# Layer ends by token halves with weights kept in the arena: a two-block model on one core

## The reference, cut to what matters

```python
def first_block(...):                      # x with 16 meta tokens ahead: 528 tokens
    ...
        h = h + _sq_relu_mlp(_rmsnorm(h, norm_mlp[layer]), mlp_w1[layer], mlp_w2[layer])
    h = _rmsnorm(h, norm_final)
    return h[:, N_META:, :]

def second_block(...):
    for l in range(DEPTH):                 # DEPTH = 2
        x = x + 0.5 * rms_norm(swiglu(rms_norm(x, nw[0]), ffn_w_gate[l, 0], ...), nw[1])
        hn = rms_norm(x, nw[2])
        m = even_mixer(hn, ...) if l % 2 == 0 else odd_mixer(hn, ...)
        x = x + rms_norm(m, nw[3])
        x = x + 0.5 * rms_norm(swiglu(rms_norm(x, nw[4]), ffn_w_gate[l, 1], ...), nw[5])
    return x
```

## Time and profile before

| | |
|---|---|
| median of 3 runs | 4032.64 us (4027.40 to 4035.25) |
| the profiled execution | 4038.64 us |
| its span | 4036.8 us |
| busy: PE / PEld / DVE / ACT / POOL | 93% / 77% / 44% / 35% / 35% |
| mean granted clock of TensorE | 0.953 of full speed |
| DMA | 307.73 MB, 76 GB/s over the span |

### The profile page before, as it was taken

How to read it: one execution, slowest core, us unless ns; L and a number is a source line. 1 busy time by engine, 2 the same in 40 slices (tenths; PEclk the granted TensorE clock), 3 DMA queues, 4 the chain that set the end, 5 groups by cost and what they waited for, 6 DMA issues and landing times.

```text
span 4036.8 us, 52115 instructions
## 1 busy us (share of the span) xinstructions
PE 3749.6 (93%) x19667; PEld 3120.2 (77%) x19667; DVE 1793.5 (44%) x2059; ACT 1234.3 (31%) x1865; POOL 1425.6 (35%) x595
## 2 busy tenths in 40 slices
PE   8888899999998899989998989998999887879998
PEld 8776799999974788868886768886888665557886
DVE  3552235446454454452336642325233489633224
ACT  3532232223134222232223432223222333533222
POOL 3221134444320244434444144444444400044444
PEclk9988899999997899999999999999999999989999
DMA  3110022222210122222222012222222222022222
GB/s 143 63 63 31 27 74 84 89 89 89 79 58 1 52 94 94 97 70 94 94 94 84 31 58 96 96 94 79 94 94 94 81 71 68 1 84 73 94 94 83
DMA packets 85401, 307.73 MB, mean 76 GB/s; under 512 B 9456, under 2 KB 9712, under 8 KB 85104
## 3 DMA queue, kind: packets, MB, share of 16 engines
q1 hardware_dynamic: 84816, 304.28, 21.6%
q10 hardware_dynamic: 416, 1.05, 0.1%
HBM read 303.19 MB, written 2.10 MB: 76 GB/s over the span
## 4 chain that ended last, share of the span: by engine, by line
issue 44%; PE 39%; POOL 14%; DVE 2%; POOLq 0%; DVEq 0%; ACT 0%; ACTq 0%
PE psum L326 37%; POOL w_lo L297 12%; POOL resid L721 2%; DVE square_sum L504 1%; PE psum L1670 1%; PE psum L1634 0%; DVE arena L944 0%; PE psum L1654 0%; PE psum L541 0%; PE psum L534 0%; DVE y_lo L932 0%; DVE arena L942 0%; POOLq L296 0%; POOLq L235 0%; DVEq L943 0%
## 5 line engine op out<-in xcount | busy, mean ns | idle before, releaser
L297 POOL TENSOR_TENSOR w_lo<-w_raw,w_hi 128x1024 fp32r<-128x1024 f32 x543 | 1356.8, 2499 | 2550.6 <-ACT w_hi L290 2550.6
L290 ACT ACTIVATE w_hi<-w_raw 128x1024 fp32r<-128x1024 f32 x567 | 600.5, 1060 | 2125.9 <-PE psum L326 2101.7
L326 PE MATMUL psum<-x_hi,w_hi 128*128 128x512 f32 (+1 forms) x2936 | 987.0, 363 | 61.9 <-DVE w_lo L2274 32.0
L326 PE MATMUL psum<-x_lo,w_hi 128*128 128x512 f32 (+1 forms) x2936 | 982.9, 361 | 0.0
L326 PE MATMUL psum<-x_hi,w_lo 128*128 128x512 f32 (+1 forms) x2936 | 977.8, 360 | 0.0
L326 PE MATMUL psum<-y_hi,w_hi 128*128 128x264 f32 (+1 forms) x2528 | 735.5, 336 | 41.1 <-DVE arena L1082 18.6
L326 PE MATMUL psum<-y_lo,w_hi 128*128 128x264 f32 (+1 forms) x2528 | 736.9, 337 | 0.0
L326 PE MATMUL psum<-y_hi,w_lo 128*128 128x264 f32 (+1 forms) x2528 | 733.5, 336 | 0.0
L326 PEld LDWEIGHTS psum<-x_hi,w_hi 128*128 128x128 f32 x2936 | 525.7, 189 | 166.7 <-DVE w_lo L2274 38.2
L326 PEld LDWEIGHTS psum<-x_lo,w_hi 128*128 128x128 f32 x2936 | 523.7, 189 | 87.2 <-issue 1.4
L326 PEld LDWEIGHTS psum<-x_hi,w_lo 128*128 128x128 f32 x2936 | 524.5, 190 | 85.5
(11 more groups left out here) (385 smaller groups left out, 3132.2 us busy)
## 6 DMA issues: line engine op xcount, KB each, us to landing
w_raw<-in_weights SPq DMA_DIRECT2D x567, 512.0 KB, 3.2
resid<-in_xT SPq DMA_DIRECT2D x8, 264.0 KB, 8.2
out_dram<-resid SPq DMA_DIRECT2D x8, 256.0 KB, 2.0
arena<-in_lru_w SPq DMA_DIRECT2D x1, 1024.0 KB, 10.3
rope_sb<-in_rope SPq DMA_DIRECT2D x1, 528.0 KB, 11.9
mats<-in_mats SPq DMA_DIRECT2D x1, 512.0 KB, 10.3
rope_sb<-in_rope ACTq DMA_DIRECT2D x1, 512.0 KB, 3.7
arena<-in_pool_inv ACTq DMA_DIRECT2D x1, 512.0 KB, 4.3
```

The source lines that it names most:

```text
L290: nc.scalar.activation(WH[:, (n + c) % 2, :], RAW[:, (n + c) % 4, :], ACT.Copy).then_inc(high_ready, 1)
L297: nc.gpsimd.tensor_tensor(WL[:, (n + c) % 2, :], RAW[:, (n + c) % 4, :], WH[:, (n + c) % 2, :], ALU.subtract).then_inc(low_ready, 1)
L326: last = mm(o[:, a, :], wt[:, ws, k * P:k * P + P], x[:, k, a * (w // banks):(a + 1) * (w // banks)], start=(k == 0 and p == 0), stop=(k = ...
```

## The change

At all seven ends the tokens are treated in two halves of 256 columns. The closing stage's first four chunks stay whole. Its last four are done for the first half of the tokens (c4 to c7, semaphore `half_done`), then, with the same weights, for the second half (`tile_done`). The first half's column sums come behind c4's second half, its spread behind c5's. The next stage's first three chunks (two before) are done by `first_halves`: eight k-steps for the first half of the tokens, then eight for the second, each with its half ones-product; the second half's sums stand behind step 2 and its spread behind step 4. For this up to five chunks' high and low parts stay in the arena (`RESIDENT`, `FREE_AT` names the chunk that must be done before). ACT splits chunks 2 to 9 in pairs ahead of the squares of tiles 0 to 3, then chunk 10, and later 11, 12 and 13. DVE adds the residual itself (`update`); `post_pool`, its semaphore and the POOL additions are gone. The output leaves in 16 halves. INV, a table of the even mixer, moves from the arena to YA. The diff, cut to its core:

```diff
+        AFTER = {"final": "f0", "f0p": "even", "evenp": "f1", "f1p": "f2", "f2p": "odd", "oddp": "f3"}
+        CLOSING = {"final": ("mlp1_down3", 8), "f0p": ("ffn0_down2", 6), "evenp": ("e_out", 8), "f1p": ("ffn1_down2", 6),
+                   "f2p": ("ffn2_down2", 6), "oddp": ("o_out_y", 8), "f3p": ("ffn3_down2", 6)}
+        RESIDENT, FREE_AT = {}, {}
+        for name, (stage, _) in CLOSING.items():
+            n = CHUNKS[stage]
+            slots5 = [(RES[:, 2 * i, :], RES[:, 2 * i + 1, :]) for i in range(5)]
+            if name == "oddp":
+                slots5 = ([(RES_A[:, 2 * i, :], RES_A[:, 2 * i + 1, :]) for i in range(2)] +
+                          [(RES_B[:, 2 * i, :], RES_B[:, 2 * i + 1, :]) for i in range(3)])
+            for i in range(5):
+                RESIDENT[n + 2 + i], FREE_AT[n + 2 + i] = slots5[i], n + (name in ("evenp", "oddp"))
+            FREE_AT[n + 7] = n + 2
+            if name in AFTER:
+                FREE_AT[n + 8], FREE_AT[n + 13] = n + 1, n + 8
+                for i in range(4):
+                    RESIDENT[n + 9 + i], FREE_AT[n + 9 + i] = slots5[i], n + 3 + i
...
+            at = n + 4 * i + c if isinstance(i, int) else None
+            if at in FREE_AT:
+                act.wait_ge(tile_done, FREE_AT[at])
+            elif n + c >= 2:
                 act.wait_ge(tile_done, 4 * i + n + c - 1)
-            nc.scalar.activation(WH[:, (n + c) % 2, :], RAW[:, (n + c) % 4, :], ACT.Copy).then_inc(high_ready, 1)
+            nc.scalar.activation(weight_parts(n, i, c)[0], RAW[:, (n + c) % 4, :], ACT.Copy).then_inc(high_ready, 1)
...
+        def half_sums_pe(pe, name, h):
+            pe.wait_ge(added, added_at(name) + (11 if h else 7))
+            for j in (2 * h, 2 * h + 1):
+                last = mm(G[:, 5, j:j + 1], ACC[:, P * j:P * j + P], ones[:, 0:1], start=True, stop=True)
+            last.then_inc(summed_up, 1)
...
+        def half_passes(n, c, k, kt, hi, lo, h):
+            wh, wl = weight_parts(n, 0, c)
+            for q, (w, x) in enumerate(((wh, hi), (wh, lo), (wl, hi))):
+                last = mm(G[:, (n + c) % 4, half(h)], w[:, k * P:k * P + P], x[:, k, half(h)],
+                          start=(k == 0 and q == 0), stop=(k == kt - 1 and q == 2))
+            return last
+        def first_halves(pe, name, n):
+            w, post = WIDE_SUMS.index(name), PRECEDING[name]
+            low_wait(pe, n + 2)
+            pe.wait_ge(psum_free, n + 3)
+            for h in range(2):
+                for k in range(DT):
+                    m = 8 * h + k
+                    pe.wait_ge(x_low, PART_AT[name] + m + 1)
+                    for c in range(3):
+                        last = half_passes(n, c, k, DT, XH, XL, h)
+                        if m == 15:
+                            last.then_inc(tile_done, 1)
+                    pe.wait_ge(prep_squared, 16 * w + m + 1)
+                    mm(G[:, 4, half(h)], ones[:, :], PREP_SQ[m % 4], start=(k == 0),
+                       stop=(k == DT - 1)).then_inc(wide_summed, 1)
+                    if m == 2:
+                        half_sums_pe(pe, post, 1)
+                    if m == 4:
+                        half_spread_pe(pe, post, 1)
...
-                split_high(act, n + 2, 0, 0)
                 act.wait_ge(wide_mean, WIDE_SUMS.index(name) + 1)
                 nc.scalar.activation(DEV, VAR, ACT.Sqrt).then_inc(wide_dev, 1)
+                split_high(act, n + 5, 0, 0)
...
+        def close_pe(pe, name, hi, lo, parts):
+            stage, kt = CLOSING[name]
+            n = CHUNKS[stage]
+            product(pe, n, 4, hi, lo, kt=kt, parts=parts)
+            for h in range(2):
+                for c in range(4, 8):
+                    if h == 0:
+                        low_wait(pe, n + c)
+                        pe.wait_ge(psum_free, n + c + 1)
+                    else:
+                        pe.wait_ge(final_tile, FINALS[name] + c + 1)
+                    for k in range(kt):
+                        last = half_passes(n, c, k, kt, hi, lo, h)
+                    last.then_inc(tile_done if h else half_done, 1)
+                    if h and c == 4:
+                        half_sums_pe(pe, name, 0)
+                    if h and c == 5:
+                        half_spread_pe(pe, name, 0)
+            if name not in AFTER:
+                half_sums_pe(pe, name, 1)
+                half_spread_pe(pe, name, 1)
...
+        def close_act(act, name, src):
+            n, last_added = CHUNKS[CLOSING[name][0]], added_at(name)
...
+            def part(m):
+                if name not in AFTER:
+                    return
+                nxt, f, c = AFTER[name], m % 8, half(m // 8)
+                act.wait_ge(updated, 16 * CLOSES.index(name) + m + 1)
+                nc.scalar.activation(XH[:, f, c], r[f][:, c], ACT.Copy, scale=prep_gain(nxt, f)).then_inc(x_high, 1)
+                if m > 3:
+                    act.wait_ge(wide_summed, 16 * WIDE_SUMS.index(nxt) + m - 3)
+                nc.scalar.activation(PREP_SQ[m % 4], r[f][:, c], ACT.Square).then_inc(prep_squared, 1)
+            for f in range(4):
+                for m in (2 * f + 2, 2 * f + 3):
+                    if n + m < N_CHUNKS:
+                        split_high(act, n + m, 0, 0)
+                tile_square(f)
...
+                split_high(act, n + 10, 0, 0)
+            for m in range(4, 9):
+                tile_square(m)
+            root(0)
+            tile_square(9)
+            part(0)
+            tile_square(10)
+            part(1)
+            tile_square(11)
+            part(2)
+            part(3)
+            root(1)
+            part(4)
+            if name in AFTER:
+                split_high(act, n + 11, 0, 0)
+            part(5)
+            part(6)
+            if name in AFTER:
+                split_high(act, n + 12, 0, 0)
+            for m in range(7, 16):
+                part(m)
...
+        def close_dve(dve, name, finish, y, g, scale):
...
+            def add(m):
+                f, c = closing_tile(m)
+                dve.wait_ge(squared, SQUARES[name] + m + 1)
+                dve.drain()
+                tt(ACC[:, c], ACC[:, c], SQ[f % 2][:, c], ALU.add).then_inc(added, 1)
...
+            def update(m):
+                f, h = m % 8, m // 8
+                c = half(h)
+                ps = G[:, 6 + h, 0:HALF]
+                if f == 0:
+                    dve.wait_ge(spread, sum_at(name, h) + 1)
+                if y is None:
+                    stt(r[f][:, c], r[f][:, c], g[f], ps, ALU.mult, ALU.mult).then_inc(updated, 1)
+                    dve.drain()
+                    return
+                t = SCR[:, 2, half(m % 2)]
+                stt(t, y[:, f, c], g[f], ps, ALU.mult, ALU.mult)
+                dve.drain()
+                tt(r[f][:, c], r[f][:, c], t, ALU.add).then_inc(updated, 1)
+            def low(m):
+                if name not in AFTER:
+                    return
+                nxt, f, c = AFTER[name], m % 8, half(m // 8)
+                dve.wait_ge(x_high, PART_AT[nxt] + m + 1)
+                stt(XL[:, f, c], r[f][:, c], prep_gain(nxt, f), XH[:, f, c], ALU.mult, ALU.subtract).then_inc(x_low, 1)
+            for m in range(8):
+                done(m)
+                if m > 1:
+                    add(m - 1)
+            add(7)
+            done(8)
+            mean(0)
+            add(8)
+            root(0)
+            done(9)
+            add(9)
+            update(0)
+            done(10)
+            add(10)
+            update(1)
+            low(0)
+            done(11)
+            add(11)
+            for m in range(2, 16):
+                update(m)
+                low(m - 1)
+                if m == 3:
+                    mean(1)
+                if m == 4:
+                    root(1)
+            dve.drain()
+            low(15)
+            dve.drain()
...
+            for m in range(2 * DT):
+                sp.wait_ge(updated, 16 * CLOSES.index("f3p") + m + 1)
+                f, c = m % DT, HALF * (m // DT)
+                sp.dma_start(out[P * f:P * f + P, c:c + HALF], H[:, f, META + c:META + c + HALF]).then_inc(out_done, 16)
+            sp.wait_ge(out_done, 16 * 2 * DT)
...
-            pool_stream(pool, at, N_CHUNKS)
-            post_pool(pool, "f3p")
+            pool_stream(pool, 0, BY_DVE[0])
+            pool_stream(pool, BY_DVE[1], N_CHUNKS)
```

274 lines of the change are left out of this document (136 added, 138 removed).

## The result

The changed kernel takes 3987.3 us (median of 3982.7 to 3997.3), the kernel before beside it 4032.4: 0.9893 of it, 95% interval 0.9871 to 0.9914. So 45 us are won where 20 were forecast; the forecast range of 3985 to 4032 holds the time near its lower end.

The account below looks back on a forecast made before the run. TensorE, busy 93%, bounds the kernel, so time is won only where it waits or runs at half clock. 10.1 + 9.0 + 10.0 + 1.4 − 0.9 − 3.0 − 4.5 − 2.2 = 19.9 us won: median 4012.7, range 3985 to 4032.

Parts of the forecast that it names:

- Prices: Assumed operation costs: half pass 0.1195 us, DVE half addition 0.43, three-operand half 0.48 or 0.40, m-pass 1.5.
- Rival 4: All half passes: they run slower than 0.1195 us; at 0.14 the time is 4054; chance 0.09.
- Rival 3: Openings wait until the whole closing is through, so half tokens don't help; about 4030; chance 0.05.
- Rival 2: 6-step ends: backlog worse or second-half statistics later, 5 us more at each of four; 4032; chance 0.14.
- 8-step closings: Ends final, evenp, oddp: no stall at the sums; 10.1, 9.0 and 10.0 us won.
- 6-step closings: f0p, f1p, f2p: 3.0 lost, 1.4 won, 0.9 lost, before 1.5 us more lost at each for the clock.
- the backlog's length: 6-step ends: POOL's nine subtractions alternate with DVE operations for 26.6 us, ending 30.2 us after the chunk's beginning.
- PE's "6.0 us": 6-step ends: PE stands 6.0 us after c4's second half, until seven square sums are added at 36.0.
- the loss by the clock: f0p, f1p, f2p: passes at half clock after the standstill cost 1.5 us each, 4.5 in all.
- f3p (forecast 2.2 lost, measured 1.5 won): Last end: sums at 30, DVE's updates of 0.98 us replace POOL's additions; 23.1 against 20.9, 2.2 us lost.
- the last output later than now: Sign at the end of the span: the final output would come later than in the kernel before.
- Rival 1: Port backlog doesn't form: 45 us more won, 3968, or 3990 with half of it; chance 0.15.

Follow-up runs that it names:

- changed, once more: The changed kernel itself run again with no edit, as the measure for the other runs: 3986.9 us.
- e9: Changed kernel with throwaway ones-products filling two TensorE waits (before c4's second half and the first half's sums) at the four 6-step ends: 3993.2 us.
- e1: Changed kernel with the residual addition moved back from DVE to POOL, by halves, at six ends: 4002.5 us.
- c3: Changed kernel with later second-half statistics, throwaway products in two waits at f0p, f1p and f2p, and POOL's residual addition at f3p alone: 3971.5 us.
- e2: Changed kernel with POOL's subtraction for the eleven chunks around each end cut from 1024 to 128 columns: 3959.3 us.

## Why the prediction was wrong in its size

The direction, the places and the mechanisms held; the ends won 40.7 us where the terms gave 19.9. Of the 20.8 between them, 10.6 lie at f0p, f1p and f2p, 6.5 at the three ends of 8 k-steps and 3.7 at f3p. By the prediction's steps:

**Prices.** Right: half additions 0.42 and 0.43, the three-operand half 0.47 or 0.48, m-passes 1.49 to 1.51 apart, a half pass 0.119 (96 of them from 1727.42 to 1738.82 at final). DVE's step was 1.29 and not 1.4. Rival 4 fell with them. Rival 3 too: the openings start while DVE still finishes the closing's last tile. Rival 2 fell because the sums came earlier than forecast, not later.

**8-step closings (forecast 10.1, 9.0, 10.0; measured 13.1, 11.6, 10.9).** No stall at the sums, as foreseen. From the end of the fourth tile at final (1727.42), the first low part was used at 24.0 (forecast 24.5), m3 at 31.6 (32.5), m6 at 38.1 (39.5), and the three chunks were through at 53.0 instead of 54.5. POOL's two subtractions cost PE 0.26 and 0.75 us there, 1.0 in all and not 1.3. (At evenp and oddp of "changed, once more" they cost about 0.8 and 1.3.)

```profile
1754.20 0.38 PE L636 MATMUL psum<-x_hi,w_hi 128*128 128x256 f32 x1 [1.01 <-DVE x_lo L892]
...
1759.03 0.39 PE L636 MATMUL psum<-x_hi,w_hi 128*128 128x256 f32 x1 [1.22 <-DVE x_lo L892]
...
1763.00 0.39 PE L636 MATMUL psum<-x_hi,w_hi 128*128 128x256 f32 x1 [0.26 <-DVE x_lo L892]
1765.51 0.39 PE L636 MATMUL psum<-x_hi,w_hi 128*128 128x256 f32 x1 [0.75 <-DVE x_lo L892]
```

About another 1.0 us lies behind the end, where I counted nothing: behind its two waits for POOL (2.07 and 1.91 us) the kernel before had a granted clock of 0.91 for 20 us of passes at final, and the same at evenp; the changed one, without them, had 1.00 at final. These waits are no sure price, though: behind the same two at f1p the kernel before had 1.00. With the 1.5 us of the chunks this leaves some 0.5 of final's 3.0 open, and of the 2.6 at evenp and 0.9 at oddp I have no such account.

```profile
1792.00:1812.00 20.00, 20.00 (x82) 16.07 (x81) 5.21 (x6) 5.38 (x7) 7.84 (x4) 0.91 0.30 106
...
2410.00:2430.00 20.00, 20.00 (x81) 16.07 (x81) 5.26 (x6) 5.37 (x7) 7.86 (x4) 0.91 0.31 106
...
2808.00:2828.00 20.00, 20.00 (x88) 16.23 (x87) 6.79 (x7) 5.37 (x7) 9.45 (x4) 1.00 0.30 106
```
```profile
1781.00:1801.00 20.00, 19.70 (x85) 15.69 (x84) 10.44 (x11) 8.67 (x11) 6.69 (x3) 1.00 0.16 53
```

**6-step closings (forecast −3.0, 1.4 and −0.9, less 1.5 each for the clock; measured −0.7, 3.0, 1.3).** The step that failed first is the backlog's length, "9 × (2.36 + 0.59) = 26.6 us". From the chunk's beginning (2706.1 at f1p) POOL was to end at 30.2 and the sums to come at 36.0; POOL ended at 28.1 and they came at 33.8. A subtraction with its handing over took 2.64 in the first five and 2.8 in the next four, not 2.95: 24.4 in all. What stands between POOL's end and the sums took 5.7 us for 5.8, as forecast. PE's "6.0 us" was 2.1 at c4's second half and 1.44 to 3.0 at the sums, 3.5 to 5.1 together. The second is the loss by the clock, added as 4.5 us on top. Filling the waits shows such a loss (e9: 1.1 to 2.0 an end), but the first low part came at 45.6 and in "changed, once more" at 44.5, where I had 45.5 before adding it: the sums that came 2.2 earlier paid for it. The opening took another 1.3 us less than forecast (76.1 for 77.4). With the 1.5 that makes 2.8 of f1p's 3.1; f0p and f2p missed by 3.8 and 3.7, and the same terms stand in them.

**f3p (forecast 2.2 lost, measured 1.5 won).** Sums at 28.8 for 30, updates at 0.89 us for 0.98, the end of the span at 54.1 for 57.7 (from the chunk's beginning at 3941.4). So the sign "the last output later than now" did not come. The last rows are DVE's, not POOL's as in the earlier trace rows; e1 and c3 show that POOL would be better there after all: 0.68 an update, with its stt beside it.

```profile
3992.34 0.47 DVE L883 SCALAR_TENSOR_TENSOR arena<-arena,vecs_sb,psum 128x256 f32<-128x256 f32 x1
3992.89 0.43 DVE L885 TENSOR_TENSOR resid<-resid,arena 128x256 f32<-128x256 f32 x1
```
```profile
3961.81 5.49 POOL L2625 TENSOR_TENSOR resid<-arena,resid 128x256 f32<-128x256 f32 x8 [0.42 <-DVE arena L893]
```

**Rival 1** said 3968 if the backlog did not form (45 us beyond the forecast) and 3990 with half of that. The time, 3987, lies where its half case lies, but not by its mechanism: all nine subtractions stood in a row, with DVE's additions at up to 3.0 us beside them. With the subtractions thinned the time is 3959 (e2), so the port still costs 28 us in the median and 32 over the stretches, 9.8, 9.7 and 7.4 at the three ends where the backlog is. The forecast had 45 for it. A time that fits a rival is no sign of its mechanism.

So each end was forecast 1 to 4 us too dear, always to the same side: where a wait was uncertain I took the late value, and added the parts as if none had slack. No single cause makes the 20.8; that the total lies inside the range is no merit of these terms. Of the 45 between the medians, the rest beside the 40.7 lies in the middle (326.0 to 324.0, different between runs) and ahead of the first end.

## What to carry to other kernels

Before moving work to shorten an idle stretch of TensorE, ask how much of its price is the slower clock behind it: throwaway products in the wait are an edit of a few lines, and here gave half of what a large restructuring gave. But fill only a wait that is there, place by place (2.3 us at one end, 0.3 at another, where the filling cost 3.1 us). A statistic that an engine must wait for belongs as late in that engine's queue as its user allows: that one move was worth 11 us, more than any other order tried.

## What the runs showed of the hardware that I had not expected

- After two waits of only 2.07 and 1.91 us, 6 us apart, the granted clock was 0.91 over the next 20 us at final and evenp of the kernel before, and 1.00 at f1p of the same run. At f1p one profile of the changed kernel had 0.50 and another 0.78 in the six microseconds around and after the same sums, 33.9 us after the chunk's beginning in both; the waits ahead were 2.10 and 2.31 us in the one, 2.09 and 2.95 in the other. The clock behind a wait is not the same from place to place, nor from run to run:

```profile
2726.00:2732.00 6.00, 3.70 (x21) 3.70 (x22) 3.50 (x10) 2.64 (x5) 0.00 (x0) 0.78 0.01 3
```

- What a DVE addition pays for meeting POOL's subtraction hardly depends on its own size: 2.61 us for 512 columns that take 0.69 alone, 2.08, 2.31 and 2.39 for 256 columns that take 0.42, so 1.9 and 1.7 to 2.0 more. Halving a tile does not halve that price.
- The first event of the same program, the finish of tile 0 at final, came between 1700.5 and 1710.9 us in two profiles, so that two runs of this kernel may differ by several us without any cause in the part that was changed.
